# Mixture-of-experts step: gate/up in two halves of the weights, the prior expert's second projection between and behind them, front rows in column tiles of 64

## The reference, cut to what matters

```python
gu = xb @ w_gate_up[e] + b_gate_up[e]          # 1024 -> 2048 columns
g = jnp.minimum(gu[:, :D_FF], SWIGLU_LIMIT)
u = jnp.clip(gu[:, D_FF:], -SWIGLU_LIMIT, SWIGLU_LIMIT)
act = (u + 1) * g * jax.nn.sigmoid(SWIGLU_ALPHA * g)
return act @ w_down[e] + b_down[e]             # 1024 -> 1024 columns
```

## Time and profile before

| | |
|---|---|
| median of 3 runs | 1725.76 us (1725.15 to 1731.21) |
| profiled execution, own time | 1725.22 us |
| its span | 1723.5 us |
| TensorE busy in the span | 1471.9 us, 85% |
| VectorE, ScalarE, GpSimd busy | 773.2, 355.5, 96.5 us |
| mean granted TensorE clock | 0.905 of full speed |
| read from HBM, rate over the span | 589.36 MB, 357 GB/s |

### The profile page before, as it was taken

How to read it: one execution, slowest core, us unless ns; L and a number is a source line. 1 busy time by engine, 2 the same in 40 slices (tenths; PEclk the granted TensorE clock), 3 DMA queues, 4 the chain that set the end, 5 groups by cost and what they waited for, 6 DMA issues and landing times.

```text
span 1723.5 us, 32057 instructions
## 1 busy us (share of the span) xinstructions
PE 1471.9 (85%) x11950; PEld 591.5 (34%) x11951; DVE 773.2 (45%) x1120; ACT 355.5 (21%) x822; POOL 96.5 (6%) x173
## 2 busy tenths in 40 slices
PE   3878886778887969899998998898999899999970
PEld 2433333345433344332332332332332232332320
DVE  2789878987886244131232132132132131131326
ACT  3212212222222111121212122112122121121220
POOL 0000011000000000000000000000000000000000
PEclk8989995679898858999999998999999999998995
DMA  9557888989998685598999999999999999999986
GB/s 328 183 189 243 296 285 275 359 296 307 313 296 287 233 338 212 228 428 339 424 423 399 417 429 379 411 427 394 402 430 412 398 427 400 410 428 385 429 367 254
DMA packets 127292, 598.10 MB, mean 347 GB/s; under 512 B 20503, under 2 KB 20517, under 8 KB 102026
## 3 DMA queue, kind: packets, MB, share of 16 engines
q1 hardware_dynamic: 109088, 560.20, 82.3%
q10 hardware_dynamic: 8634, 20.00, 3.4%
q0 software_dynamic: 9504, 17.06, 2.6%
HBM read 589.36 MB, written 25.87 MB: 357 GB/s over the span
## 4 chain that ended last, share of the span: by engine, by line
PE 41%; DMA 20%; issue 1%; SPq 0%; DVE 0%; ACT 0%; ACTq 0%; DVEq 0%
PE pair L1517 25%; DMA wts<-in_w_gate_up 16%; PE bank L1554 8%; PE bank L1536 4%; DMA wts<-in_w_down 3%; DMA wts<-y_rows 1%; PE bank L1507 1%; PE bank L1624 1%; PE bank L1565 1%; PE bank L1605 0%; DVE v_ring L2148 0%; DMA h_tok<-h_rows,v_tok 0%; ACT k_T L1161 0%; SPq L646 0%; SPq L657 0%
## 5 line engine op out<-in xcount | busy, mean ns | idle before, releaser
L1517 PE MATMUL pair<-wts,h_T 128*32 128x512 f32 x4032 | 443.9, 597 | 9.6 <-DMA wts<-in_w_gate_up 5.0
L2070 DVE TENSOR_SCALAR q_T<-pair 128x512 f32<-128x512 f32 x32 | 22.1, 692 | 638.9 <-PE pair L1517 638.9
L1517 PEld LDWEIGHTS pair<-wts,h_T 128*32 128x32 f32 x4032 | 129.6, 111 | 307.9 <-issue 297.1
L1554 PE MATMUL bank<-wts,k_T 128*32 128x512 f32 x2048 | 228.3, 596 | 6.4 <-issue 4.9
L1536 PE MATMUL bank<-wts,h_T 128*32 128x512 f32 x992 | 133.1, 676 | 54.4 <-DMA wts<-in_w_gate_up 52.6
L1664 DVE TENSOR_TENSOR wts<-wts,q_b 128x1024 f32<-128x1024 f32 x128 | 158.0, 1234 | 23.3 <-DMA wts<-in_cache_k 17.6
L1667 DVE TENSOR_REDUCE sc<-wts 128x16 f32<-128x1024 f32 x128 | 156.2, 1220 | 4.4
L1151 ACT ACTIVATE h_T<-bank 128x512 f32<-128x512 f32 x66 | 35.9, 595 | 575.8 <-PE bank L1507 575.8
L1554 PEld LDWEIGHTS bank<-wts,k_T 128*32 128x32 f32 x2048 | 65.9, 110 | 146.3 <-issue 137.8
L1229 PE MATMUL pair<-wts,h_T 128*8 128x128 f32 (+1 forms) x480 | 96.0, 476 | 12.1 <-ACT h_T L860 6.4
L1161 ACT ACTIVATE k_T<-bank 32x256 f32<-32x256 f32 x256 | 95.7, 374 | 13.6 <-PE bank L1554 10.2
(11 more groups left out here) (333 smaller groups left out, 1411.0 us busy)
## 6 DMA issues: line engine op xcount, KB each, us to landing
wts<-in_w_gate_up SPq DMA_DIRECT2D x126, 2048.0 KB, 15.7
wts<-in_w_down SPq DMA_DIRECT2D x64, 2048.0 KB, 18.2
wts<-in_cache_k SPq DMA_DIRECT2D x256, 256.0 KB, 3.8
v_ring<-in_cache_v SPq DMA_DIRECT2D x160, 256.0 KB, 3.8
wts<-in_cache_v SPq DMA_DIRECT2D x96, 256.0 KB, 3.9
wts<-in_w_in SPq DMA_DIRECT2D x5, 2048.0 KB, 24.1
wts<-y_rows SPq DMA_DIRECT2D x4, 2048.0 KB, 15.1
wts<-in_w_out ACTq DMA_DIRECT2D x8, 512.0 KB, 6.6
```

Source lines behind the costliest of these rows:

```text
L1517: m = nc.tensor.matmul(PS[part][p0:p0 + 32, :], lhs[:, 32 * b:32 * b + 32], rhs[:, part * F + half * 512:part * F + half * 512 + 512], sta ...
L1554: m = nc.tensor.matmul(PS[4][p0:p0 + 32, :], act_T[0][:, k, a0:a0 + 32], chunk[c][:, k, n * 512:(n + 1) * 512], start=(c == 0 and k == 0), ...
```

## The change

Gate/up is cut at the weights: half 0 takes chunks 0 and 1, half 1 takes chunks 2 and 3 and the bias. In each half the back parts come first, then the front. Chunk 4's share of the second projection of expert i-1 stands between the halves, chunk 5's share behind half 1 and the token transposes; a second back part (over 96 rows) takes both its chunks at the first of these places. SyncE loads in the same order: 0, 1, 4, 2, 3, 5. The front products use 64 token rows and 64 output partitions each where they used twice 32; the back products stay at 32. The sizes of both experts are read at the head of the block.

```diff
--- before.py
+++ after.py
...
-            def load_gate_up(i, e):
-                for c in range(4):
-                    sp.wait_ge(w_used[c], i)
-                    load_chunk(c, e)
-
-            def load_down(i, e):
-                for c in range(4, 6):
-                    sp.wait_ge(w_used[c], i)
-                    load_chunk(c, e)
+            def load_used(c, i, e):
+                sp.wait_ge(w_used[c], i)
+                load_chunk(c, e)
...
             for c in range(2):
-                sp.wait_ge(w_used[c], 2)
-                load_chunk(c, e)
-            load_down(1, 1)
+                load_used(c, 2, e)
+            for c in range(4, 6):
+                load_used(c, 1, 1)
             with sp.Fori(3, E) as i:
-                load_gate_up(i, expert_at(i))
-                load_down(i - 1, expert_at(i - 1))
+                for c in range(2):
+                    load_used(c, i, expert_at(i))
+                load_used(4, i - 1, expert_at(i - 1))
+                for c in range(2, 4):
+                    load_used(c, i, expert_at(i))
+                load_used(5, i - 1, expert_at(i - 1))
...
-            def gate_up_front(i, chunk=gu_chunk):
+            def gate_up_front(i, half, chunk=gu_chunk):
 
                 def products(lhs, rhs, start, stop):
                     for part in range(2):
                         for half in range(2):
-                            for b in range(2):
-                                p0 = 64 * half + 32 * b
-                                m = nc.tensor.matmul(PS[part][p0:p0 + 32, :], lhs[:, 32 * b:32 * b + 32],
-                                                     rhs[:, part * F + half * 512:part * F + half * 512 + 512],
-                                                     start=start, stop=stop)
+                            m = nc.tensor.matmul(PS[part][64 * half:64 * half + 64, :], lhs[:, 0:64],
+                                                 rhs[:, part * F + half * 512:part * F + half * 512 + 512],
+                                                 start=start, stop=stop)
                     return m
 
-                for c in range(4):
+                for c in range(2 * half, 2 * half + 2):
                     pe.wait_ge(w_full[c], i * 16 + 16)
                     for k in range(2):
                         m = products(hg_T[:, 2 * c + k, :], chunk[c][:, k, :], c == 0 and k == 0, False)
                     m.then_inc(w_used[c], 1)
-                pe.wait_ge(sel_done, i + 1)
-                products(sel[0:96, :], b_split[0:96, :], False, True).then_inc(gu_done, 1)
-
-            def gate_up_back(i, b, chunk=gu_chunk):
+                if half:
+                    pe.wait_ge(sel_done, i + 1)
+                    products(sel[0:96, :], b_split[0:96, :], False, True).then_inc(gu_done, 1)
+
+            def gate_up_back(i, b, half, chunk=gu_chunk):
 
                 def products(lhs, rhs, start, stop):
                     for part in range(2):
@@ -1537,63 +1534,55 @@
                                              rhs[:, part * F + half * 512:part * F + half * 512 + 512],
...
-                for c in range(4):
+                for c in range(2 * half, 2 * half + 2):
                     pe.wait_ge(w_full[c], i * 16 + 16)
                     for k in range(2):
                         products(hg_T[:, 2 * c + k, :], chunk[c][:, k, :], c == 0 and k == 0, False)
-                pe.wait_ge(sel_done, i + 1)
-                products(sel[0:96, :], b_split[0:96, :], False, True)
-
-            def down_front(i, chunk=dn_chunk, full=w_full[4:6], loads=0):
-                for c in range(2):
-                    pe.wait_ge(full[c], i * 16 + 16 * (loads + 1))
-                    for k in range(4):
-                        for n in range(2):
-                            for b in range(2):
-                                p0, a0 = 64 * n + 32 * b, 64 * c + 32 * b
-                                m = nc.tensor.matmul(PS[4][p0:p0 + 32, :], act_T[0][:, k, a0:a0 + 32],
-                                                     chunk[c][:, k, n * 512:(n + 1) * 512],
-                                                     start=(c == 0 and k == 0), stop=(c == 1 and k == 3))
-                    m.then_inc(w_used[4 + c], 1)
-
...
+                if half:
+                    pe.wait_ge(sel_done, i + 1)
+                    products(sel[0:96, :], b_split[0:96, :], False, True)
+
+            def down_front(i, c, chunk=dn_chunk, full=w_full[4:6], loads=0):
+                pe.wait_ge(full[c], i * 16 + 16 * (loads + 1))
+                for k in range(4):
+                    for n in range(2):
+                        m = nc.tensor.matmul(PS[4][64 * n:64 * n + 64, :], act_T[0][:, k, 64 * c:64 * c + 64],
+                                             chunk[c][:, k, n * 512:(n + 1) * 512],
                                              start=(c == 0 and k == 0), stop=(c == 1 and k == 3))
...
+                m.then_inc(w_used[4 + c], 1)
+
+            def down_back(i, b, c, chunk=dn_chunk, full=w_full[4:6], loads=0):
+                pe.wait_ge(full[c], i * 16 + 16 * (loads + 1))
+                for k in range(4):
+                    a0 = 64 * b + 32 * c
...
+            def size_of(i):
+                return pe.value_load(n_tok[0:1, bass.ds(i, 1)], min_val=0, max_val=CAP)
+
+            def by_size(size, front, back):
+
                 with pe.If(size > 64):
-                    back(i, 0)
+                    back(0)
                     with pe.If(size > 96):
-                        back(i, 1)
-                front(i)
-                return size
+                        back(1)
+                front()
+
+            def gate_up(i, size, half, chunk=gu_chunk):
+                by_size(size, lambda: gate_up_front(i, half, chunk), lambda b: gate_up_back(i, b, half, chunk))
+
+            def down(i, size, c, chunk=dn_chunk, full=w_full[4:6], loads=0):
+
+                with pe.If(size > 64):
+                    if c == 0:
+                        with pe.If(size > 96):
+                            for q in range(2):
+                                down_back(i, 1, q, chunk, full, loads)
+                    down_back(i, 0, c, chunk, full, loads)
+                down_front(i, c, chunk, full, loads)
...
-            def expert_block(i, before=None, front=gate_up_front, back=gate_up_back):
+            def expert_block(i, before=None, chunk=gu_chunk):
+
+                size = size_of(i)
+                size_before = None if before is None else size_of(before)
                 after(pe, gclip_done, i * 2)
                 pe.wait_ge(xt_copied, i * 2 + 2)
-                size = by_size(front, back, i)
+                gate_up(i, size, 0, chunk)
+                if isinstance(i, int) and i == 1:
+                    pe.wait_ge(late_slots_done, 1)
+                if before is not None:
+                    down_ready(before, isinstance(i, int))
+                    down(before, size_before, 0)
+                gate_up(i, size, 1, chunk)
                 transpose_x(i + 1)
                 if isinstance(i, int) and i == 0:
                     enter_late()
-                if isinstance(i, int) and i == 1:
-                    pe.wait_ge(late_slots_done, 1)
                 if before is not None:
-                    down_block(before, isinstance(i, int))
+                    down(before, size_before, 1)
                 for part in range(2):
                     pe.wait_ge(xt_copied, i * 2 + (part + 3))
                     pe.wait_ge(act_done, i * 2 + (part + 1))
@@ -1626,12 +1622,11 @@
                     m.then_inc(at_full, 1)
                 return size
 
-            def down_block(i, first, front=down_front, back=down_back, size=None):
+            def down_ready(i, first):
                 pe.wait_ge(at_copied, i * 2 + 2)
                 if not first:
                     pe.wait_ge(y_front, i)
                     pe.wait_ge(y_back, i)
-                by_size(front, back, i, size)
...
-            expert_block(1, 0, first_gate_up_front, first_gate_up_back)
+            expert_block(1, 0, first_gu)
             with pe.Fori(2, E) as i:
                 expert_block(i, i - 1)
-            down_block(E - 1, False, last_down_front, last_down_back)
+            size = size_of(E - 1)
+            down_ready(E - 1, False)
+            for c in range(2):
+                down(0, size, c, last_dn, last_full)
```

More of the change, by code:

```diff
@@ L648, in _ @@
                     e = expert_at(j + E)
-                    load_gate_up(j + E, e)
-                    load_down(j + E, e)
+                    for c in range(6):
+                        load_used(c, j + E, e)
             sp.wait_ge(y_scattered, (n + E) * 16)
@@ new lines, in down_back @@
+            def down_back(i, b, c, chunk=dn_chunk, full=w_full[4:6], loads=0):
+                pe.wait_ge(full[c], i * 16 + 16 * (loads + 1))
+                for k in range(4):
+                    a0 = 64 * b + 32 * c
```

(8 more changed lines are left out.)

23 lines of the change are left out of this document (removed).

## The result

| | before | changed |
|---|---|---|
| median | 1726.55 us (4 runs) | 1793.88 us (4 runs, 1792.75 to 1796.94) |
| ratio to before | | 1.040, 95% interval 1.0381 to 1.0418 |
| span of the profiled execution | 1723.5 us | 1791.1 us |
| mean granted TensorE clock | 0.905 | 0.89 |

A forecast was written before the change was run, and what follows sets the result against it. Weight transfers and TensorE's products alternate, neither alone being the bound. Blocks 6 to 28 at -14, blocks 1 to 5 at +4 and the end at -3.5 took 1725.2 to 1711.7 us, median 1712; range 1694 to 1740.

The forecast's parts named there:

- big blocks starve the queue: Weight loads: big blocks free nothing for 16 us, SyncE's queue runs dry; transfers lose 31 us over blocks 6 to 28.
- Wide products at no change: Front products of 64 rows: same time as twice 32 rows, at 0.213 us pitch.
- Changes of tile width at 0.15 us each: Switches between 32-row and 64-row products around big experts: 0.15 us each, 0.9 per pair; upper end 0.25, 1.5 per pair.
- VectorE's chain is what is late next: Ahead of the activation transposes: TensorE idles 2.3 us after a small expert, 0.6 after a big one, in two pieces.
- TensorE's side of a pair: A small and a big block together: 60.6 + 0.9 for widths + 0.6 for reads = 62.1 us, against the transfers' 61.4.
- Control: Size reads and branches at the block's head: a second read may add 0 to 1.2 us; taken as 0.3 per block.
- The prediction's own signs of being wrong: Front pitch above 0.22 us, head gap above 0.5 us, or granted clock falling in more than one block of four.
- The rival on the clock: VectorE's two new gaps let TensorE's clock fall, 1.5 us per fall, in two of three blocks: 1742 us; chance 0.16.
- The transfers' floor of 706 us: Blocks 6 to 28: 302 MB at 428 GB/s need 706 us; rival with transfers running through, 1695 us, chance 0.18.
- +4 was forecast: Blocks 1 to 5, ahead of block 6: together 4 us slower.
- So they are there: Block 29 to the loop's last front product: 12 chunks arrive in time, 77.2 us instead of 80.7, -3.5.

The follow-up runs named there:

- run 1: Kernel before the change with only its front products widened to 64 rows; 1721.37 us against 1725.39, ratio 0.998.
- run 2: Changed kernel with its front products back at 32 rows twice, new order kept; 1796.31 us, ratio 1.0405.
- run 8: Changed kernel with the second projection whole behind both gate/up halves, loads 0 to 5, front products back at 32 rows twice; 1711.60 us, ratio 0.9927.
- run 3: Changed kernel with both sizes held in registers, the next block's size read ahead of the activation waits; 1722.56 us, ratio 0.998.
- run 6: Changed kernel with the second projection whole behind both gate/up halves, its size read there, loads 0 to 5; 1713.67 us, repeated 1713.36 us.
- run 4: Changed kernel with only this block's size read at the head, the prior expert's size in a register; 1749.30 us, ratio 1.0134.
- run 5: Changed kernel with two extra 512-column products ahead of each of two waits for VectorE, both reads at the head; 1764.96 us, ratio 1.0228.

## Why the prediction was wrong

**What bounds the kernel before, and that big blocks starve the queue: right in kind.** With chunks freed by halves the waits for weights went in the changed kernel, at first sight for nothing. With the cover restored the earlier freeing gives 0.7%, though TensorE waits for weights again there.

**Wide products at no change: right** (runs 1, 2, 8). In run 3's timeline 32 take from 1258.36 to 1265.38, 0.219 us each with the change of width behind them; the forecast was 0.213. The Trainium skill's page TensorEngine Tiling (Array Packing), Available Configurations, which lists 128x64 as two tiles, is borne out; the rule for outputs of 32 partitions alone, in the Trainium skill's TensorE: Matmul & The Clock Gate, What picks the tile position, is not a limit here.

**Changes of tile width at 0.15 us each: right.** Runs 6 and 8 differ in the width of the front products alone. Block 7, with a big expert's second projection and so three changes more, takes 27.46 us in run 6 (875.06 to 902.52) and 27.02 in run 8 (868.15 to 895.17); block 3, without back products, takes 23.59 and 23.57. That is 0.14 to 0.15 per change, 0.9 per pair. In run 2 it does not show: the pair takes 68.20 there (1241.07 to 1309.27) against 68.25, since its slow first products take 9.09 us instead of 8.72 and a part of what TensorE saves is spent waiting for VectorE. The Trainium skill's page TensorEngine Tiling (Array Packing), Key Properties, says that a change drains the engine; the price of 0.25 us that the prediction worked out for such a drain, 1.5 per pair, was too high.

**VectorE's chain is what is late next: right**, with 1.14 and 0.89 us where about 1.3 and 0.8 stood in the forecast. TensorE's side of a pair was put at 62.1 us. Run 3, which has every part of the change but the reads at the head, has 1286.50 - 1224.54 = 61.96 in a pair without a fall of the clock.

**The step that failed is "Control": 0.3 us per block, measured 1.7.** The row for a read with its branch, at most 1.18 us behind a signal, is not contradicted. The rest of the step took the second read alone as exposed, "nearer to nothing since no gap stands at any block's head now". But that absence of a gap came from cover: in block 18 of the kernel before, VectorE's last signal is at 1263.31 + 0.69 and block 19 starts at 1265.88, 1.9 us for one read of 1.18. The text's own term before it had just taken that cover away and left 0.6 us of transposes. With the numbers at hand: signal to first product 1.18 + 1.2 for the second read = 2.4, against 0.7, a gap of 1.7, which is what the changed kernel and run 2 show (the changed kernel: signal at 1302.57 + 0.69, first product at 1305.91, 2.65 us). The prediction's own signs of being wrong, a head gap over 0.5 us and a fall of the clock in more than one block of four, both came. Signal of VectorE, changed kernel:

```profile
1302.57 0.69 DVE L1664 TENSOR_TENSOR rot<-qk,rot 128x512 f32<-128x512 f32 x1
```

Two reads stood behind the one wait that the change had made the last to end, and everything of the next block queued behind them. In blocks 6 to 28 run 3 is 788.1 - 725.4 = 62.7 us shorter than the changed kernel. The head gaps are 32.8 us of that (38.0 to 5.2 over 23 heads, 1.4 each), the first products at full speed 32.4, and against them stand 3.0 us of waits for weights that come up.

**The rival on the clock was right in its size and right in part in its condition.** 1.5 us per fall were priced, 1.6 and 1.7 are measured. The prediction had it set off by VectorE's two gaps, with a chance of 0.16, against it a row with gaps of 0.92 and 2.96 us at full speed. Those two gaps with hardly any behind them do it at four of eleven heads (run 3), with a head gap of about 1.0 behind them at all eleven (run 4); gaps of 0.22 and 0.90 do it at none (run 4), 0.23 and 1.65 at all (changed kernel), and without VectorE's gaps it never falls (run 5). At the frequency of run 3 the rival would have cost about 7 us in these blocks; the mis-sized head gap made it the rule. The Trainium skill's warning against idle gaps between bursts (TensorE: Matmul & The Clock Gate, Why this matters for your kernels) agrees in kind; here it is several short gaps, none over 1.8 us, with products between them. It adds to the first loss rather than standing as a rival to it.

**The transfers' floor of 706 us was too low.** It took 428 GB/s, from a window of 32 us, for the whole. Run 6, in which TensorE waits for weights in each block from 9 on, has 0.99 DMA share and 414 GB/s, and its blocks 6 to 28 take 1571.14 - 843.96 = 727.2 us, 63.2 per pair and not 61.4. The change could win 9 to 11 us in that stretch (727.2 in run 6, 725.4 in run 3, 736.4 before), not the 31 of the floor.

**Even with the control term right the forecast was 9 us too low.** Run 3's profiled execution took 1720.6 us against 1711.7, and its timeline says where:

```profile
849.45 3.64 PE L1533 MATMUL bank<-wts,h_T 128*32 128x512 f32 x32 [0.18 <-issue]
...
1574.88 7.09 PE L1513 MATMUL pair<-wts,h_T 128*64 128x512 f32 x32 [0.28 <-issue]
...
1615.16 3.65 PE L1513 MATMUL pair<-wts,h_T 128*64 128x512 f32 x16 [1.44 <-DMA wts<-in_w_gate_up]
1620.78 5.35 PE L1513 MATMUL pair<-wts,h_T 128*64 128x512 f32 x16 [1.96 <-DMA wts<-in_w_gate_up]
...
1651.41 3.65 PE L1513 MATMUL pair<-wts,h_T 128*64 128x512 f32 x16 [0.91 <-DMA wts<-in_w_gate_up]
...
1656.52 3.65 PE L1549 MATMUL bank<-wts,k_T 128*64 128x512 f32 x16
```

Block 6 starts 0.2 us earlier than before, where +4 was forecast. The eleven pairs from block 6 to the start of block 28, at 1539.17, take (1539.17 - 849.45)/11 = 62.7 us each, as forecast (62.6), four falls of the clock included; all of blocks 6 to 28 take 725.4, 3.4 over the forecast. The end is the larger miss: from block 29's start to the last front product 1656.52 + 3.65 - 1574.88 = 85.3 us, forecast 77.2. "So they are there" was wrong of the chunks; TensorE waits 4.3 us for them and the clock falls twice. Behind that, VectorE's two gaps of 2.0 us stand once more ahead of the last second projection, which the sum left out. Together -4.2 + 3.4 + 8.1 + 2.0 = 9.3 us.

What stays open: why the same two gaps let the clock fall at four heads of run 3 and not at seven. And why the rate of the transfers falls to 398 GB/s in a big block's gate/up. Fewer loads in the queue there would fit, and so would the scatter of a big expert's rows; no run tells them apart.

## What to carry to other kernels

When a change shortens the work that lies behind a wait, price again everything that runs in that shadow, the sequencer's register reads and branches first: "no gap now" is a statement on the cover, not on the cost. Read loop-carried values ahead of the last wait, not behind it. On TensorE a small gap next to others can cost more than itself, since the granted clock can halve behind it. And free a buffer early without touching the order of the work that covers another engine's chain: here that is 0.7% faster, where the interleaving was 4% slower with the reads at the head and level without them.

## What the runs showed of the hardware that was not expected

- A read of a size from SBUF into a TensorE register costs 0.7 to 0.75 us where nothing covers it (head gaps of 0.14 to 0.32 us with none, 0.86 to 1.04 with one, 1.34 to 1.80 with two, over blocks 7 to 29).
- The same gaps of 1.14 and 0.89 us ahead of the transposes let the granted clock fall at four heads of run 3 and leave it at 1.00 at seven.
- Adding four full-width products to every block made the kernel 29 us faster, 1793.88 to 1764.96, by keeping the granted clock at 1.00 and by covering the reads.
- A change between 32-row and 64-row tiles costs 0.14 to 0.15 us (runs 6 and 8).
- A DMA share of 1.0 does not fix the rate: 398 and 426 GB/s both stand at 0.98 to 1.00.
